# A state-space stage: VectorE's chunk states ahead of the convolution of the tile in hand

## The reference, cut to what matters

```
xbc = silu(causal_depthwise_conv(xbc, conv_w, conv_b))       # 4 taps
xs, bm, cm = split(xbc)
dt = softplus(dt_raw + dt_bias);  a_cs = cumsum(dt * a)       # within a chunk
cb = einsum('bclgn,bcsgn->bclsg', cm, bm)
scores = cb * decay * dt
y_diag = einsum(scores, xs)
states = einsum('bcsgn,bcsgr,bcsgrp->bcgrpn', bm, decay_end * dt, xs)
h[c+1] = chunk_decay * h[c] + states                          # over the chunks
y_off = einsum('bclgn,bcgrpn->bclgrp', cm, h_prev) * exp(a_cs)
y = (y_diag + y_off + d_skip * xs) * silu(z)                  # then a norm per group
```

## Time and profile before

| what | value |
|---|---|
| median of 3 runs | 2653.79 us (2652.95 to 2657.43) |
| profiled execution | 2652.92 us, of which 2651.2 us are the span of the trace |
| PE busy, whole span | 2496.6 us (94%) |
| DVE busy, whole span | 1709.4 us (64%) |
| state-space stage, 496 to 800 us of the span | PE busy 282.96 us, DVE 243.94, ACT 167.89 |

### The profile page before, as it was taken

One profiled execution on the slowest core, in us unless ns is written; L12 is line 12 of the kernel. 1 busy time (PEld: TensorE's weight loads), 2 busy tenths in 40 slices (PEclk: granted clock), 3 DMA queues, 4 the chain that ended last, 5 costly groups with the idle time before them and its releaser, 6 DMA issues. The chain is left out here.

```text
span 2651.2 us, 33863 instructions
## 1 busy us (share of the span) xinstructions
PE 2496.6 (94%) x13321; PEld 1983.7 (75%) x13321; DVE 1709.4 (64%) x2444; ACT 1167.7 (44%) x1705; POOL 63.1 (2%) x166
## 2 busy tenths in 40 slices
PE   7999899999999999899988899999999889999998
PEld 5666678777777877788875457888888877788886
DVE  4788445588875666899966566677766664632435
ACT  5555522255564235688853334522324143531323
POOL 0000000000000001000001000000000000000000
PEclk9999999999999988999999999999999889999999
DMA  7888627233335724999962203234332423233321
GB/s 264 271 289 282 222 85 283 81 106 93 85 99 202 257 50 174 352 420 418 418 249 92 78 27 104 80 119 135 111 112 83 120 78 130 66 107 98 96 80 32
DMA packets 299502, 427.44 MB, mean 161 GB/s; under 512 B 27690, under 2 KB 213533, under 8 KB 289488
## 3 DMA queue, kind: packets, MB, share of 16 engines
q1 hardware_dynamic: 289424, 395.13, 43.7%
q0 software_dynamic: 5392, 20.97, 2.0%
q10 hardware_dynamic: 4528, 9.18, 0.9%
HBM read 384.11 MB, written 41.14 MB: 160 GB/s over the span
## 5 line engine op out<-in xcount | busy, mean ns | idle before, releaser
L3738 PE MATMUL banks<-big,late_parts 128*128 128x512 f32 x1920 | 440.3, 391 | 4.3 <-PEq L151 3.8
L3738 PEld LDWEIGHTS banks<-big,late_parts 128*128 128x128 f32 x1920 | 361.4, 188 | 81.8 <-issue 6.1
L3738 PE MATMUL banks<-h_parts_second,late_parts 128*128 128x512 f32 x1440 | 329.8, 389 | 4.7 <-DVE h_parts_second L3950 4.7
L3738 PEld LDWEIGHTS banks<-h_parts_second,late_parts 128*128 128x128 f32 x1440 | 270.2, 188 | 61.0 <-issue 5.1
L3926 DVE TENSOR_TENSOR late_parts<-w_second,late_parts 128x2048 fp32r<-128x2048 f32 x69 | 158.1, 2292 | 216.0 <-ACT late_parts L3811 215.8
L2393 DVE TENSOR_TENSOR expert_parts<-w,expert_parts 128x2048 fp32r<-128x2048 f32 x102 | 232.8, 2289 | 22.1 <-ACT expert_parts L2389 21.6
L3811 ACT ACTIVATE late_parts<-w_second 128x2048 fp32r<-128x2048 f32 x69 | 132.0, 1914 | 253.3 <-PE banks L3738 253.2
L1358 PE MATMUL banks<-h_parts,ssm_parts 128*128 128x512 f32 x960 | 228.8, 395 | 0.6 <-DVE ssm_parts L1625 0.4
L2389 ACT ACTIVATE expert_parts<-w 128x2048 fp32r<-128x2048 f32 x102 | 194.8, 1917 | 61.9 <-PE banks L2400 52.2
L1358 PEld LDWEIGHTS banks<-h_parts,ssm_parts 128*128 128x128 f32 x960 | 178.4, 188 | 42.9 <-issue 6.1
L2400 PE MATMUL banks<-expert_parts,expert_xt 128*128 128x512 f32 x816 | 191.6, 394 | 4.2 <-DVE expert_xt L2381 4.2
(11 more groups left out here) (703 smaller groups left out, 3858.7 us busy)
## 6 DMA issues: line engine op xcount, KB each, us to landing
w_second<-in_mlp_w_dram SPq DMA_DIRECT2D x64, 1024.0 KB, 5.3
w<-in_w_exp_gate_dram SPq DMA_DIRECT2D x34, 1024.0 KB, 9.1
w<-in_w_exp_up_dram SPq DMA_DIRECT2D x34, 1024.0 KB, 8.9
w<-in_w_exp_down_dram SPq DMA_DIRECT2D x34, 1024.0 KB, 8.9
w<-in_w_in_dram SPq DMA_DIRECT2D x64, 512.0 KB, 4.6
w<-in_mod_mix_w_dram SPq DMA_DIRECT2D x24, 1024.0 KB, 5.1
w<-in_mod_ffn_w_dram SPq DMA_DIRECT2D x23, 1024.0 KB, 5.3
w<-in_w_in_dram SPq DMA_DIRECT2D x16, 1024.0 KB, 5.6
```

Of the source, the lines that this page charges most:

```text
L3738: mm = pe.matmul(ps[:, bank(n, f), :], w_part(n, w)[:, kk, f * P:(f + 1) * P], x[:, v, kk, :], start=(first_chunk(n) and kk == 0 and j == ...
```

## The change

In groups 0 to 2 VectorE takes the low part of tile t + 2 first, then the chunk states, and only then the convolution of tile t - 1 and the silu of tile t - 2. No instruction is added or taken away, and the lists of the other engines stay as they are.

```diff
                 mask_products(i)
                 dve.wait_ge(s["cb_ready"], i + 1)
                 scores(i, 0)
-                tile_at(i, 3)
+                if more(i, 3) is not None:
+                    low(more(i, 3) + 2)
                 states(i)
+                if more(i, 3) is not None:
+                    follow(more(i, 3))
                 if i:
                     normalise(i - 1, range(KG))
                 for f in range(KG):
```

## The result

The changed kernel took 2659.18 us (median of 18 runs, 2653.99 to 2664.05) against 2654.77 us before (18 runs, 2652.73 to 2660.97). The ratio is 1.0015, with a 95% interval from 1.0008 to 1.0022: slower by some 4 us, and within the 0.2% that was called no change. The forecast was 2656.5 us in a range from 2652.5 to 2660.0.

The account below looks back on a forecast made before the run. VectorE was taken to bound the stretch from the states to the scores of heads 2 and 3, PE the rest. Terms -0.3 + 1.5 + 1.5 = +2.7 us gave 2655.6 profiled, 2656.5 us as median; range 2652.5 to 2660.0.

Parts of the forecast that it names:

- The first waits: PE's waits for the states at heads 0 and 1, groups 0 to 2: 2.36, 2.42 and 2.42 us, all to vanish.
- the covers of 1.1 us (ScalarE's high part) and 1.2 us (PE at the heads): Slack in the new order: high part ends 1.1 us before the low part starts; states ready 1.2 us before PE arrives.
- They return at heads 2 and 3: PE would instead wait for VectorE's scores there: some 2.0, 4.66 and 4.65 us; groups 1 and 2 gain nothing.
- VectorE's unbroken stretch: From before the states until after the scores of heads 2 and 3, VectorE has no idle time, so that time stays.
- Group 0 gains 0.3 us: Without normalisation ahead of the scores, heads 2 and 3 of group 0 could start at 576.75 instead of 577.08.
- The moved convolution costs nothing by itself: Later tanh, high part and exponents on ScalarE cost nothing; group 0's exponents keep 0.5 us to spare.
- The clock falls behind both long waits, at 1.5 us each: PE's clock drops after the 4.65 us waits at heads 2 and 3, groups 1 and 2: +1.5 us each; chance 0.57.
- The sum: Whole kernel: -0.3 + 1.5 + 1.5 = +2.7 us on the profiled execution.
- The rival "slower": Each long wait's clock drop costs 2.9 us and group 0's wait drops it too: +7.0 us, 2660.8 us; chance 0.08.
- The third drop: Clock also falling behind group 0's 2.0 us wait at heads 2 and 3, 1.5 us, claimed only by the slower rival.
- The rival "faster": All three waits at heads 0 and 1 won and kept: 7.2 us gained, 2646.6 us; chance 0.03.

Follow-up runs that it names:

- e4: Changed kernel with the normalisation of the group before moved behind the scores of heads 4 and 5 in groups 1 and 2; 0.9994 against the kernel before.
- g3: Changed kernel with the low part left behind the convolution, VectorE taking the states first; 1.0005 against the kernel before.
- f2: Changed kernel with small filler matmuls on PE in all three moved waits (7 in group 0, 18 in groups 1 and 2); 1.0004 against the kernel before.
- g2: Same kernel as f2, run again on another chip; 1.0008 against the kernel before.
- f1: Changed kernel measured again, unaltered, on a second chip; 1.0009 against the kernel before.
- g1: Changed kernel measured a third time, unaltered, on a third chip; 1.0013 against the kernel before.
- after: Profile of the changed kernel itself, unaltered; that execution took 2653.99 us.
- e1: Changed kernel with 18 small filler matmuls on PE in front of heads 2 and 3 in groups 1 and 2 only; 1.0007 against the kernel before.
- e2: The change in group 0 alone, groups 1 and 2 as in the kernel before; 1.0003 against the kernel before.
- f3: Changed kernel with normalisation moved into VectorE's idle time and ScalarE's first square behind the last exponents, groups 1 and 2; 0.9971 against the kernel before.
- f4: Same as f3 plus 7 small filler matmuls in each wait of heads 2 and 3, groups 0 to 2; 0.9963 against the kernel before.

## Why the prediction held

*The first waits go.* As predicted, at once and in all three groups; the covers of 1.1 us (ScalarE's high part) and 1.2 us (PE at the heads) were enough.

*They return at heads 2 and 3.* Predicted 2.0, 4.66 and 4.65 us; measured 1.96, 4.69 and 4.70. The reason, VectorE's unbroken stretch, is shown by e4, where less work in front of the scores brought the heads forward by as much, and by g3, where another order of the same work did not.

*Group 0 gains 0.3 us.* Measured 0.4 (24.42 to 24.00).

*The moved convolution costs nothing by itself.* ScalarE's exponents came later, and VectorE waited for none; the last one in group 0 ended at 575.25 and was taken at 575.70, 0.45 us later, where 0.5 was forecast. With the clock held up (f2, g2) the stage is 0.5 us shorter than before.

*The clock falls behind both long waits, at 1.5 us each.* It fell in all three profiles of the changed kernel, behind six waits of six (once, in f1, only 1 us after the wait had ended, which cost 661.90 - 652.99 - 7.36 = 1.6 us). The price is the term that was mis-sized. From heads 2 and 3 to heads 4 and 5 it took 662.27 - 652.93 = 9.34 and 740.47 - 730.83 = 9.64 us, against 584.39 - 577.03 = 7.36 in group 0 at full clock: 2.0 and 2.3 us. The 1.5 was taken from heads that were slow alone; here the clock stayed low into the tile behind them. The sum becomes -0.4 + 2.0 + 2.3 = +3.9, and the stage shows +3.8. Over the six drops the price lay between 1.6 and 2.4 us, inside the bounds of nothing and 2.9 that were set for it.

*The total.* +4.4 us between the medians, +2 to +6 by the interval (f1 and g1: +2.1 and +3.1 between the medians). The forecast stood 2.7 us too low: 1.0 of that is the median of three runs that it started from (2653.79, where 18 runs gave 2654.77), 1.2 the price, and 0.5 stays unexplained. The rival "slower" needed 2.1 us for each long wait and one more drop in group 0. The price reached that (2.0 and 2.3). The third drop stayed away: of the seven profiles that have the wait of some 2.0 us in group 0 without fill (after, f1, g1, e1, e2, e4, f3) only e1 shows it, at 1.6 us. That the range held with so low a forecast was in part luck, for the median lies 0.8 us under its upper end, and one more drop in most runs would have carried it past. The rival "faster" failed where it was said to: VectorE had no idle time to give.

The rule of the Trainium skill that was weighed (page "TensorE: Matmul & The Clock Gate", section "HAM oscillation — how this bites in real kernels"), a cost of half of the time at the low clock, agrees here: 4.3 and 4.8 us of matmuls at 0.50 cost 2.0 and 2.3 us, and half of them is 2.15 and 2.4.

## What to carry to other kernels

Before an engine's list is reordered to release PE sooner, look for its next wait on the same engine: where that engine is busy without a break between the two, the wait only moves, and work has to leave the stretch for it to shrink. Two short waits joined into one long one can cost more than the two, because the clock falls behind it and what follows then lies on the path. Work that is moved out belongs in idle time that the trace shows, behind whatever another engine takes next from the same list.

## What the runs showed that I had not expected

The clock fell during the long waits and outlasted them: with PE idle from 648.3 us, it was at 0.52 from 650.3 and at 0.50 until 657.2. A wait of about 2 us is no safe length either. In f3 the clock fell behind both such waits in groups 1 and 2, in e4 behind one of two; behind that of group 0 it never fell in the profiles of the changed kernel, and in e1 it did. With fills of 1.6 us in such waits it did not fall in the profiles that had them (group 0 in f2 and g2, all three groups in f4). The whole kernel's scatter goes with the clock too: the kernel before took 2649.95 to 2664.90 us in 35 runs on one chip, its fastest run at a mean granted clock of 0.977, its slowest at 0.970.
